# The causal mask moved from TensorE into VectorE's row maximum, and ten heads' decay falls moved from ScalarE to GpSimd

## The chip, the cores and the metric

The kernel runs on one core of a Trainium2 chip. The metric is the device time of one execution in microseconds (us). TensorE, VectorE (DVE), ScalarE (ACT) and GpSimd (POOL) each take their instructions in program order, and SyncE (SP) issues the loads and stores.

## The reference

One step of a hybrid decoder layer: latent attention with 8 heads and a Mamba-2 mixer with 16 state-space heads read the same normalised input (512 prompt tokens and 8 sample tokens, width 1024). What the change touches:

```python
# attention of the prompt, by head and by block of 128 queries
sc = (q_lat @ ckv.T + q_rope @ k_rope.T) * SOFTMAX_SCALE
sc = where(k_pos <= q_pos, sc, NEG_BIG)          # the causal mask
p  = softmax(sc)                                 # exp(sc - row maximum) / row sum
# state-space heads, chunks of 128 tokens; a_cum is the running sum of dt * a
decay_in = exp(a_cum[l] - a_cum[s]) for s <= l, else 0
y_diag   = (C B^T * decay_in) @ xdt
# then y = (y_diag + y_off + d * xs) * silu(z), and an RMSNorm over each group of 8 heads
```

## The kernel before, in words

The order of the work is written out by hand for each engine; semaphores join the engines. There are four stages: the first loads and first two weight tiles (0 to 15 us), the projections (to 279 us, with the sample tokens' paged attention woven in), the state-space states and the value matrices (to 312 us), the loop over the attention heads (312 to 397 us), and the output projection (to the end).

**First stage.** SP loads `xraw` tile by tile and the pieces 1 to 3 of the first two weight tiles; ACT's queue loads `cols` and piece 0 of both. PE runs six f32 matmuls on a zeroed tile before `first_two`. Each weight tile is split into `w_hi` (ACT, `hi`) and `w_lo` (DVE, `lo`), and PE's item i waits for `w_lo` of item i. `norm_total(0)` (L1842) sums the squares over the partitions, and ACT's `root(0, r_pre)` makes the norm's factor from it; ACT does this at i == 1, ahead of `hi(4)`.

**Head loop.** Iteration s of `for s in range(H - 1)` on every engine:

- PE: `scores(s+1)` for blocks 0, 1 and 2, the transposes `probs_t(s, 0)` and `probs_t(s, 1)` (L2067), `scores(s+1)` block 3, one `y_pair` of state-space heads (L2019, L2022; two in iteration 1, none in 6), `keys(s+2)` (L2043), and `outs(s, 0..3)` (L2075) between the last transposes. A block's scores are `kn` (f32, L2056), the mask (`ident_r` by `mask_r`, 128 columns, L2057) and two rope parts (L2058, L2059). The three PSUM banks of scores go round, so block 3 waits until ACT's `exps(s+1, 0)` has read block 0.
- DVE: `mask_max` (L1451, a row maximum in PSUM), `inverse_sum` (L1457), `head` (L1396, the decay times C B^T), `state_update` (L1416) and `dots` (L1424, a multiply and row sum with accumulator) of the sample states, `mix_low` (L1469), `y_pair` (L1404, L1405, L1406), and `gated` (L1465) last.
- ACT: `exps` (L917), the copies of `pt` and `kn`, `mix_high`, `gated_square` (L658), `state_decay` (L893), and `decays(h)`: four Relu with a bias, 128x128 each (L883), then one Exp of 128x512 (L886).
- POOL: `norm` (L1688, probabilities by the inverse row sum), `gate(t)` (L1694) and `add_square(t)` (L1705).

The decay tiles `dec` are loaded by SP (`load_acb`) once an earlier `y_pair` on PE has freed the slot. Behind the loop DVE has the chain `group_scale(0..3)` (L1480), `lo(NIN)`, `mix_low(6)`, `gated(7)`, `lo(NIN+1)`, `ssm_low(0)`, `mix_low(7)`, and PE's first output item needs its weights and, at its eighth tile, `mix_low(7)`.

Of the kernel before, what the change touches and what calls it, by code (L numbers as in the profile page):

```python
# [19 lines left out]
P = 128  # L20
# [49 lines left out]
M_ID, M_ONE, M_TRI, M_MQ, M_ML = range(5)  # L70
# [34 lines left out]
STATE_DECAYS = {0: (1,), 1: (2,), 2: (3,), 3: (4,), 4: (5,)}  # L105
# [19 lines left out]
def build(nc, a):  # L125
# [95 lines left out]
    for name, shape in (("cm", [P, 5, P]), ("cols", [P, NCOL]), ("rows", [P, 2, SH]), ("qlp", [P, 2, NB, 32 + ROWS]),  # L221
# [8 lines left out]
        if name == "cm":  # L230
            CM_ = o
        if name == "qlp":
            dxs = at("dxs", [P, 2, 8, NB], F, o)
            orow = at("orow", [P, 2 * P], F, o + 2048)
# [24 lines left out]
    nmh, alpha, rs, epsc, nmx, rsum = (small[k] for k in ("nmh", "alpha", "rs", "epsc", "nmx", "rsum"))  # L259

    ident_r = at("ident_r", [P, P], R, CM_ + 4 * P * M_MQ)
    mask_r = at("mask_r", [P, P], R, CM_ + 4 * P * M_ML)

# [29 lines left out]
    a_mask, a_gf, a_out = sem("mask_rounded"), sem("group_factor_done"), sem("out_copied")  # L293
# [97 lines left out]
    def _(sp):  # L391
# [234 lines left out]
    def _(act):  # L626
# [143 lines left out]
        for i in range(2):  # L770
            act.dma_start(w_raw[i][:, 0:256], a["w_in"][i][:, 0:256]).then_inc(s_w0[0], 16)
# [22 lines left out]
        for i in range(NIN):  # L794
# [30 lines left out]
            if i == 1:  # L825
                root(0, r_pre)
# [51 lines left out]
        def decays(h):  # L878

            act.wait_ge(s_acb[h % 6], 16 * (h // 6 + 1))  # L880
            for c in range(NCH):
                x = dec[h % 6][:, CH * c:CH * c + CH]
                last = act.activation(x, x, ACT.Relu, bias=acum[:, SH * c + h:SH * c + h + 1], scale=-1.0)  # L883
            last.then_inc(a_fall, 1)
            act.wait_ge(a_fall, h + 1)
            act.activation(dec[h % 6], dec[h % 6], ACT.Exp, scale=-1.0).then_inc(a_dec, 1)  # L886
# [23 lines left out]
        def exps(h, b):  # L910
# [6 lines left out]
            act.activation(pr[:, h % 2, i0:i0 + n], px[:, n_ % 3, 0:n], ACT.Exp, bias=nmx[:, k:k + 1], accum_out=rsum[:, k:k + 1])\  # L917
# [58 lines left out]
        for s in range(H - 1):  # L976
            exps(s + 1, 0)
            exps(s + 1, 1)
            copy_pt(s, 0)
            exps(s + 1, 2)  # L980
# [3 lines left out]
            if s in (1, 2):  # L984
                gated_square(SQUARES[s][0])
# [5 lines left out]
            if 3 <= s < 6:  # L991
                gated_square(SQUARES[s][0])
# [4 lines left out]
            if s == 6:  # L997
                gated_square(SQUARES[s][0])
# [8 lines left out]
            if s in (1, 2):  # L1007
                gated_square(SQUARES[s][1])
            for n in STATE_DECAYS.get(s, ()):
                state_decay(n)  # L1010
# [50 lines left out]
    def _(dve):  # L1061
# [471 lines left out]
        for s in range(H - 1):  # L1533
# [18 lines left out]
            if s < 6:  # L1552
                inverse_sum(s + 1, 2)
            if s in PAIRS:
                y_pair(PAIRS[s][0])
            for h in MASKS[1].get(s, ()):
                head(h)
            inverse_sum(s + 1, 3)
            if s == 6:
                group_scale(0)  # L1560
                group_scale(1)
            if s == 0:
                state_update(s)
            if s < 6:
                dots(s)
            gated(s)
# [72 lines left out]
    def _(pool):  # L1639
# [49 lines left out]

        def gate(t):  # L1690
# [19 lines left out]
        for s in range(H - 1):  # L1710
            norm(s + 1, 0)
            norm(s + 1, 1)
            for t in GATES[0].get(s, ()):
                gate(t)
            norm(s + 1, 2)
# [38 lines left out]
    def _(pe):  # L1754
# [205 lines left out]
        for _ in range(6):  # L1960
# [85 lines left out]
        def scores(h, blocks):  # L2046
            pe.wait_ge(a_ring, RING_AT["k", h] + 1)
            pe.wait_ge(v_qsl, STACK_AT[h])
            if h == 0:
                pe.wait_ge(a_mask, 2)  # L2050
                pe.wait_ge(v_krl, 1)
            for b in blocks:
# [4 lines left out]
                pe.matmul(px[:, n % 3, P * b:w], ident_r, mask_r, start=False, stop=False)  # L2057
# [139 lines left out]
def laid_out(x_prompt, x_sample, cache_ckv, cache_krope, state_conv, state_ssm, page_table, norm_pre, w_in,  # L2197
# [47 lines left out]
    out["cm"] = np.stack([ident, ones, low.T, np.where(low > 0, f(0), f(NEG)), np.where(low.T > 0, f(0), f(NEG))], 1)  # L2245
# [48 lines left out]
```

## Time and profile before

| what | us |
|---|---|
| median of 3 runs | 506.93 (506.39 to 507.68) |
| the profiled execution, its own time | 506.42 |
| span of the profile (first to last instruction) | 504.6 |
| PE busy in the span | 493.4 |
| DVE, ACT, POOL busy | 345.6, 293.4, 86.2 |
| granted TensorE clock, mean | 1.00 |

The 1.8 us between the span and the execution's own time lie outside the profile. A record of PE includes its pipelined end, so the distance from start to start tells its pace better than its duration.

### The profile page before, as it was taken

What the parts mean: (1) busy time and instruction counts of PE and PEld (TensorE: products, weight loads), DVE (VectorE), ACT (ScalarE), POOL (GpSimd) and SP (SyncE); (2) the same over time, 40 slices, a digit from 0 to 9 for tenths busy, and PEclk for the clock granted to TensorE, in tenths of its full rate; (3) what the DMA queues carried; (4) which work ended last, traced back from release to release, by engine and by line L of the source; (5) the groups of instructions that cost most, each with busy time, mean ns of one, the idle gap of its engine ahead of it and who ended that gap; (6) DMA issues with size and microseconds to landing.
All of it is one profiled execution on the core that took longest, in us unless ns stands there. A gap on an engine that the chain in (4) does not pass through costs nothing.

```text
span 504.6 us, 12857 instructions
## 1 busy us (share of the span) xinstructions
PE 493.4 (98%) x5002; PEld 440.3 (87%) x5002; DVE 345.6 (68%) x758; ACT 293.4 (58%) x616; POOL 86.2 (17%) x104
## 2 busy tenths in 40 slices
PE   8999999999999999999999999999999999999996
PEld 7999999999999998999999775666666699999994
DVE  5543768693856566644523698799997899996642
ACT  6543412234376473664616985689996879674532
POOL 1631000020010010000000132244554302110520
PEclk9999999999999999999999999999999999999999
DMA  8534223469898998989886542737435777889712
GB/s 307 197 128 150 81 65 103 132 212 357 280 332 281 308 294 286 326 278 332 298 279 185 60 130 49 255 92 123 142 95 184 229 251 230 296 270 376 242 58 84
DMA packets 58975, 105.72 MB, mean 210 GB/s; under 512 B 7722, under 2 KB 27859, under 8 KB 58787
## 3 DMA queue, kind: packets, MB, share of 16 engines
q1 hardware_dynamic: 58482, 104.59, 65.3%
q8 instruction: 40, 0.66, 0.5%
q10 hardware_dynamic: 432, 0.31, 0.2%
q14 instruction: 21, 0.16, 0.1%
HBM read 95.62 MB, written 7.76 MB: 205 GB/s over the span
## 4 chain that ended last, share of the span: by engine, by line
PE 80%; DVE 9%; ACT 6%; issue 3%; DMA 1%; SPq 0%; POOL 0%; DVEq 0%; ACTq 0%; POOLq 0%
PE pm L1757 17%; PE pm L1758 16%; PE pm L1759 16%; PE px L1868 3%; PE px L2056 3%; PE pm L2043 3%; PE px L1893 3%; PE pm L2075 3%; DVE w_lo L1077 2%; DVE u L1170 1%; PE px L2019 1%; PE pm L2022 1%; PE pm L2067 1%; ACT w_hi L641 1%; PE px L2058 1%
## 5 line engine op out<-in xcount | busy, mean ns | idle before, releaser
L1757 PE MATMUL pm<-xw_hi,w_lo 128*128 128x260 f32 x520 | 150.7, 290 | 0.9 <-DVE w_lo L1077 0.9
L1758 PE MATMUL pm<-xw_lo,w_hi 128*128 128x260 f32 x520 | 147.1, 283 | 0.0
L1759 PE MATMUL pm<-xw_hi,w_hi 128*128 128x260 f32 x520 | 146.9, 283 | 0.0
L641 ACT ACTIVATE w_hi<-w_raw 128x1024 fp32r<-128x1024 f32 (+1 forms) x70 | 72.4, 1037 | 73.2 <-PE pm L1759 61.0
L1077 DVE TENSOR_TENSOR w_lo<-w_raw,w_hi 128x1024 fp32r<-128x1024 f32 (+1 forms) x70 | 86.6, 1242 | 38.0 <-ACT w_hi L641 37.8
L1757 PEld LDWEIGHTS pm<-xw_hi,w_lo 128*128 128x128 f32 x520 | 98.0, 188 | 2.7 <-DVE w_lo L1077 1.1
L1758 PEld LDWEIGHTS pm<-xw_lo,w_hi 128*128 128x128 f32 x520 | 97.9, 188 | 0.1
L1759 PEld LDWEIGHTS pm<-xw_hi,w_hi 128*128 128x128 f32 x520 | 97.9, 188 | 0.0
L1757 PE MATMUL pm<-mix_hi,w_lo 128*128 128x260 f32 x224 | 63.8, 285 | 0.1
L1759 PE MATMUL pm<-mix_hi,w_hi 128*128 128x260 f32 x224 | 63.3, 283 | 0.0
L1757 PEld LDWEIGHTS pm<-mix_hi,w_lo 128*128 128x128 f32 x224 | 42.2, 188 | 0.6 <-DVE mixlo_a L1469 0.3
L1759 PEld LDWEIGHTS pm<-mix_hi,w_hi 128*128 128x128 f32 x224 | 42.2, 188 | 0.0
L761 ACT ACTIVATE alpha<-nmh 128x1 f32<-128x1 f32 x16 | 4.7, 295 | 56.1 <-DVE nmh L1183 56.1
L1170 DVE SCALAR_TENSOR_TENSOR u<-xbc,cols,u 128x511 f32<-128x511 f32 (+2 forms) x36 | 27.0, 750 | 7.0 <-ACT u L704 6.1
L1758 PE MATMUL pm<-mixlo_s,w_hi 128*128 128x260 f32 x112 | 31.7, 283 | 0.0
L1758 PE MATMUL pm<-mixlo_a,w_hi 128*128 128x260 f32 x112 | 31.6, 283 | 0.0
L1104 DVE TENSOR_TENSOR z<-pm,r_pre 128x260 f32<-128x260 f32 x32 | 13.5, 426 | 25.0 <-PE pm L1759 24.9
L1678 POOL TENSOR_TENSOR xdte<-xdt,toend 128x512 f32<-128x512 f32 x8 | 9.8, 1231 | 110.5 <-DVE xdt L1378 110.5
L1670 POOL COPY xlast<-xbc 128x11 f32<-128x11 f32 x12 | 6.0, 502 | 132.4 <-DVE xbc L1104 132.4
L1688 POOL TENSOR_SCALAR pr<-pr,rsum 128x128 f32<-128x128 f32 (+3 forms) x32 | 19.4, 606 | 49.4 <-DVE rsum L1457 48.7
L2056 PE MATMUL px<-kn,q 128*128 128x128 f32 (+3 forms) x64 | 23.1, 443 | 0.8 <-ACT pr L917 0.8
L1416 DVE SCALAR_TENSOR_TENSOR hring<-bcs,dxs,hring 128x128 f32<-128x128 f32 x64 | 23.1, 422 | 0.0
(314 smaller groups left out, 1081.9 us busy)
## 6 DMA issues: line engine op xcount, KB each, us to landing
page<-in_cache SPq DMA_DIRECT2D x128, 288.0 KB, 4.2
w_raw<-in_w_in SPq DMA_DIRECT2D x32, 512.0 KB, 5.5
w_raw<-in_w_out SPq DMA_DIRECT2D x32, 512.0 KB, 4.7
dec<-ac_dram SPq DMA_DIRECT2D x16, 256.0 KB, 10.0
hring<-in_ssm_state SPq DMA_DIRECT2D x8, 512.0 KB, 8.2
o_ssms<-hring SPq DMA_DIRECT2D x8, 512.0 KB, 6.7
w_raw<-in_w_qb SPq DMA_DIRECT2D x6, 384.0 KB, 2.9
xraw<-in_xT SPq DMA_DIRECT2D x8, 260.0 KB, 4.8
```

Source lines behind the costliest of these rows:

```text
L641: act.activation(w_hi[s][:, 0:n], w_raw[s][:, 0:n], ACT.Copy).then_inc(a_whi, 1)
L1077: dve.tensor_tensor(w_lo[s][:, 0:n], w_raw[s][:, 0:n], w_hi[s][:, 0:n].bitcast(F), ALU.subtract)\
L1170: last = dve.scalar_tensor_tensor(b[:, s:NT], xbc[:, t, 0:NT - s], col(C_CW + 4 * t + 3 - s), b[:, s:NT], ALU.mult, ALU.add)
L1416: dve.scalar_tensor_tensor(hring[b][:, t, :], bcs[b % 2][:, g, :], dxs[:, 0, t, b:b + 1], hring[b][:, t, :], ALU.mult, ALU.add).then_inc(v ...
L1688: pool.tensor_scalar(x, x, rsum[:, k:k + 1], 0.0, ALU.mult, ALU.add).then_inc(g_n, 1)
L1757: pe.matmul(out, wl, xh, start=start, stop=False)
L1758: pe.matmul(out, wh, xl, start=False, stop=False)
L1759: return pe.matmul(out, wh, xh, start=False, stop=stop)
L1868: last = pe.matmul(px[32 * j:32 * j + 32, n % 2, 64 * half:64 * half + 64], w, pages[s][:, j, c:c + 64], start=op == 0, stop=op == 4)
L1893: last = pe.matmul(px[32 * j:32 * j + 32, 3, 0:KVR], ptb[:, n % 2, c:c + 32], pages[page_slot(2 * n + half)][:, j, 0:KVR], start=half == 0 ...
L2043: last = pe.matmul(out, w_uk[:, h % 2, r, :], ckv[:, r, 0:NT], start=r == 0, stop=r == 1)
L2056: pe.matmul(px[:, n % 3, 0:w], q[:, h, P * b:P * b + P], kn[:, h % 2, 0:w], start=True, stop=False)
```

## The change

- The mask's matmul L2057 is gone (32 of them), and with it the two rounding activations on ACT and two of the five matrices in `cm`. A new tile `over` (128x512: zeros, then the triangle of -1e30) is loaded by SP after page 16, ahead of the second decay load. `mask_max` becomes one `tensor_tensor_reduce` over the block: it writes -(score + mask) back to PSUM in place and accumulates the minimum; `exps` takes the scores with scale -1.
- For heads 6 to 15 the four subtractions (`fall`) run on POOL; ACT keeps the Exp and waits for them. A fall stands at the start and at the end of POOL's iterations 1 to 4, one at the end of iteration 0, and two at the end of iteration 1.
- The order in the loop: POOL's gates and additions stand between `norm(s+1, 1)` and `norm(s+1, 2)`; the additions 6 and 7 come after the loop. DVE does `inverse_sum(s+1, 2)` and `y_pair` ahead of `mix_low` and `head`, then `state_update`, `dots`, `gated`; in iteration 6 `gated` stands ahead of `group_scale(0)` and `(1)`. ACT does `state_decay` ahead of `exps(s+1, 2)`, and all squares after `mix_high`.
- At the start: five dummy matmuls, not six; piece 0 of the first weights goes to SP's queue behind `xraw[0]`; `root(0, r_pre)` stands behind `hi(4)` (i == 2).

```diff
-SQUARES = {1: (0, 1), 2: (2, 3), 3: (4,), 4: (5,), 5: (6,), 6: (7,)}
-GATES = {1: (1,), 2: (3,)}, {0: (0,), 1: (2,), 2: (4,), 3: (5,), 4: (6,), 5: (7,)}
-ADDS = {1: (1,), 2: (2,), 3: (3,), 4: (5,), 5: (6,), 6: (7,)}
+SQUARES = {1: (0,), 2: (1,), 3: (2, 3), 4: (4,), 5: (5,), 6: (6,)}
+GATES = {0: (0,), 1: (1,), 2: (2, 3), 3: (4,), 4: (5,), 5: (6,)}
+ADDS = {2: (1,), 3: (2,), 4: (3,), 5: (5,), 6: (6,)}
...
+            if k == 0:
+                for i in range(2):
+                    sp.dma_start(w_raw[i][:, 0:256], a["w_in"][i][:, 0:256]).then_inc(s_w0[0], 16)
...
+        sp.dma_start(over, a["over"]).then_inc(s_over, 16)
...
-            if i == 1:
+            if i == 2:
                 root(0, r_pre)
...
+            else:
+                act.wait_ge(g_fall, h - 5)
+                act.activation(dec[h % 6], dec[h % 6], ACT.Exp).then_inc(a_dec, 1)
...
-            dve.tensor_reduce(nmx[:, 4 * (h % 2) + b:4 * (h % 2) + b + 1], x[:, 0:P * (b + 1)], AX.X, ALU.max,
-                              negate=True).then_inc(v_m, 1)
+            dve.tensor_tensor_reduce(x, x, over[:, NT - w:NT], -1.0, -NEG, ALU.add, ALU.min,
+                                     nmx[:, 4 * (h % 2) + b:4 * (h % 2) + b + 1]).then_inc(v_m, 1)
...
+        def fall(h):
+
+            pool.wait_ge(s_acb[h % 6], 16 * (h // 6 + 1))
+            for c in range(NCH):
+                x = dec[h % 6][:, CH * c:CH * c + CH]
+                last = pool.tensor_scalar(x, x, acum[:, SH * c + h:SH * c + h + 1], 0.0, ALU.subtract, ALU.min)
+            last.then_inc(g_fall, 1)
...
         for s in range(H - 1):
+            if s == 6:
+                pool.wait_ge(v_dot, 24)
+                gate(7)
+            for h in FALLS[s][0] if s in FALLS else ():
+                fall(h)
             norm(s + 1, 0)
             norm(s + 1, 1)
-            for t in GATES[0].get(s, ()):
+            for t in GATES.get(s, ()):
                 gate(t)
+            if s < 6:
+                for t in ADDS.get(s, ()):
+                    add_square(t)
             norm(s + 1, 2)
             norm(s + 1, 3)
-            for t in GATES[1].get(s, ()):
-                gate(t)
-            for t in ADDS.get(s, ()):
-                add_square(t)
+            for h in FALLS[s][1] if s in FALLS else (6,) if s == 0 else ():
+                fall(h)
+        add_square(6)
+        add_square(7)
...
-        for _ in range(6):
+        for _ in range(5):
...
-                pe.matmul(px[:, n % 3, P * b:w], ident_r, mask_r, start=False, stop=False)
```

## Rows read from the trace of the kernel before

**Rows 1.** Page, busy times; window table: PE, PEld, DVE, ACT, POOL, clock, DMA.
```profile
PE 493.4 (98%) x5002; PEld 440.3 (87%) x5002; DVE 345.6 (68%) x758; ACT 293.4 (58%) x616; POOL 86.2 (17%) x104
...
360.00:370.00 10.00, 10.00 (x58) 6.80 (x52) 9.00 (x26) 9.03 (x29) 4.98 (x6) 1.00 0.49 103
```

**Rows 2.** PE's timeline in the head loop: start, duration, instruction.
```profile
318.37 0.39 PE L2056 MATMUL px<-kn,q 128*128 128x128 f32 x2
...
354.13 0.39 PE L2056 MATMUL px<-kn,q 128*128 128x128 f32 x2
...
357.76 1.10 PE L2056 MATMUL px<-kn,q 128*128 128x512 f32 x2 [0.25 <-ACT pr L917]
...
376.50 0.39 PE L2056 MATMUL px<-kn,q 128*128 128x128 f32 x2
376.64 0.31 PE L2057 MATMUL px<-mask_r,ident_r 128*128 128x128 f32 x1
376.78 0.28 PE L2058 MATMUL px<-kr_lo,qs 128*128 128x128 f32 x1
376.89 0.28 PE L2059 MATMUL px<-kr_hi,qs 128*128 128x128 f32 x1
...
379.70 1.02 PE L2056 MATMUL px<-kn,q 128*128 128x512 f32 x2
...
388.30 0.38 PE L2056 MATMUL px<-kn,q 128*128 128x128 f32 x2
```

**Rows 3.** PE's waits over the whole span: total, times, longest.
```profile
PE pm L1757 <- DVE w_lo L1077: 0.9, 1, 0.9
PE px L2056 <- ACT pr L917: 0.8, 3, 0.4
```

**Rows 4.** Timelines of POOL, ACT, DVE and PE from 20 to 32 us.
```profile
20.17 6.45 POOL L1661 TENSOR_TENSOR sqs<-sqs,sqb 128x520 f32<-128x520 f32 x4
...
29.36 1.99 ACT L641 ACTIVATE w_hi<-w_raw 128x1024 fp32r<-128x1024 f32 x2
...
30.45 1.23 DVE L1077 TENSOR_TENSOR w_lo<-w_raw,w_hi 128x1024 fp32r<-128x1024 f32 x1 [5.78 <-ACT w_hi L641]
...
31.73 0.39 PE L1757 MATMUL pm<-xw_hi,w_lo 128*128 128x260 f32 x1 [0.88 <-DVE w_lo L1077]
```

**Rows 5.** The chain that ended last, at the start: start, time, what.
```profile
1.61 5.31 PE px L1962 x12
6.92 0.48 PE pm L1808 x4
```

**Rows 6.** DVE's timeline in iteration 3, and one row without POOL beside it.
```profile
369.16 1.26 DVE L1416 SCALAR_TENSOR_TENSOR hring<-bcs,dxs,hring 128x128 f32<-128x128 f32 x4
...
372.29 0.75 DVE L1404 SCALAR_TENSOR_TENSOR xbc<-xbc,cols,px 128x512 f32<-128x512 f32 x1 [0.53 <-PE pm L2022]
...
375.01 0.30 DVE L1424 CUSTOM_DVE_ANT_0 prod<-hring,bcs 128x128 f32<-128x128 f32 x1
...
375.24 0.68 DVE L1424 CUSTOM_DVE_ANT_0 prod<-hring,bcs 128x128 f32<-128x128 f32 x1
...
375.86 1.35 DVE L1424 CUSTOM_DVE_ANT_0 prod<-hring,bcs 128x128 f32<-128x128 f32 x1
...
416.93 1.14 DVE L1416 SCALAR_TENSOR_TENSOR hring<-bcs,dxs,hring 128x128 f32<-128x128 f32 x4
```

**Rows 7.** POOL's timeline in iteration 3, and its 128x128 scalings as a group.
```profile
368.82 1.20 POOL L1688 TENSOR_SCALAR pr<-pr,rsum 128x128 f32<-128x128 f32 x2 [1.41 <-DVE rsum L1457]
...
375.76 1.29 POOL L1694 TENSOR_TENSOR xbc<-xbc,z 128x512 f32<-128x512 f32 x1
...
L1688 POOL TENSOR_SCALAR pr<-pr,rsum 128x128 f32<-128x128 f32 x8 | 3.0, 372 | 20.0 <-DVE rsum L1457 20.0
```

**Rows 8.** DVE's timeline behind the head loop.
```profile
394.76 1.85 DVE L1480 SCALAR_TENSOR_TENSOR xbc<-xbc,cols,r_pre 128x512 f32<-128x512 f32 x2
...
403.02 0.69 DVE L1469 TENSOR_TENSOR mixlo_a<-u,mix_hi 128x512 fp32r<-128x512 f32 x1
```

More of the change, by code:

```diff
@@ L68 @@
 NCOL = 98
-M_ID, M_ONE, M_TRI, M_MQ, M_ML = range(5)
+M_ID, M_ONE, M_TRI = range(3)
 T_E0, T_E1 = range(2)
@@ L220, in build @@
     small = {}
-    for name, shape in (("cm", [P, 5, P]), ("cols", [P, NCOL]), ("rows", [P, 2, SH]), ("qlp", [P, 2, NB, 32 + ROWS]),
+    for name, shape in (("cm", [P, 3, P]), ("dxs", [P, 2, 8, NB]), ("cols", [P, NCOL]), ("rows", [P, 2, SH]), ("qlp", [P, 2, NB, 32 + ROWS]),
                         ("qr", [P, NB, 32]), ("ckbc", [P, 2, KVR]), ("olT", [P, 2, 2, P]),
@@ L229, in build @@
         small[name] = at(name, shape, F, o)
-        if name == "cm":
-            CM_ = o
         if name == "qlp":
-            dxs = at("dxs", [P, 2, 8, NB], F, o)
+            over = at("over", [P, NT], F, o)
             orow = at("orow", [P, 2 * P], F, o + 2048)
@@ L259, in build @@
     nmh, alpha, rs, epsc, nmx, rsum = (small[k] for k in ("nmh", "alpha", "rs", "epsc", "nmx", "rsum"))
-    ident_r = at("ident_r", [P, P], R, CM_ + 4 * P * M_MQ)
-    mask_r = at("mask_r", [P, P], R, CM_ + 4 * P * M_ML)
+    dxs = small["dxs"]
     def col(c):
@@ L878, in decays @@
         def decays(h):
[L880 to L886, printed above, removed]
+            if h < 6:
+                act.wait_ge(s_acb[h % 6], 16)
+                for c in range(NCH):
+                    x = dec[h % 6][:, CH * c:CH * c + CH]
+                    last = act.activation(x, x, ACT.Relu, bias=acum[:, SH * c + h:SH * c + h + 1], scale=-1.0)
+                last.then_inc(a_fall, 1)
+                act.wait_ge(a_fall, h + 1)
+                act.activation(dec[h % 6], dec[h % 6], ACT.Exp, scale=-1.0).then_inc(a_dec, 1)
+            else:
+                act.wait_ge(g_fall, h - 5)
+                act.activation(dec[h % 6], dec[h % 6], ACT.Exp).then_inc(a_dec, 1)
         def state_decay(n):
@@ L916, in exps @@
             i0, n, k = poff(b), P * (b + 1), 4 * (h % 2) + b
-            act.activation(pr[:, h % 2, i0:i0 + n], px[:, n_ % 3, 0:n], ACT.Exp, bias=nmx[:, k:k + 1], accum_out=rsum[:, k:k + 1])\
+            act.activation(pr[:, h % 2, i0:i0 + n], px[:, n_ % 3, 0:n], ACT.Exp, bias=nmx[:, k:k + 1], scale=-1.0, accum_out=rsum[:, k:k + 1])\
                .then_inc(a_p, 1)
@@ L983, in _ @@
                 mix_high(s - 1)
-            if s in (1, 2):
-                gated_square(SQUARES[s][0])
+            for t in SQUARES.get(s, ()):
+                gated_square(t)
             if s in FALLS:
@@ L1545, in _ @@
             mask_max(s + 1, 3)
+            if s < 6:
+                inverse_sum(s + 1, 2)
+            if s in PAIRS:
+                y_pair(PAIRS[s][0])
             if s:
@@ L1558, in _ @@
             inverse_sum(s + 1, 3)
+            if s < 6:
+                state_update(s)
+                dots(s)
+            gated(s)
             if s == 6:
@@ L1561, in _ @@
                 group_scale(1)
[L1562 to L1566, printed above, removed]
             if s == 1:
@@ L1688, in norm @@
             pool.tensor_scalar(x, x, rsum[:, k:k + 1], 0.0, ALU.mult, ALU.add).then_inc(g_n, 1)
+        def fall(h):
+            pool.wait_ge(s_acb[h % 6], 16 * (h // 6 + 1))
+            for c in range(NCH):
+                x = dec[h % 6][:, CH * c:CH * c + CH]
+                last = pool.tensor_scalar(x, x, acum[:, SH * c + h:SH * c + h + 1], 0.0, ALU.subtract, ALU.min)
+            last.then_inc(g_fall, 1)
         def gate(t):
@@ L2244, in laid_out @@
     low = np.tril(ones)
-    out["cm"] = np.stack([ident, ones, low.T, np.where(low > 0, f(0), f(NEG)), np.where(low.T > 0, f(0), f(NEG))], 1)
+    out["cm"] = np.stack([ident, ones, low.T], 1)
+    out["over"] = np.concatenate([np.zeros((P, NT - P), f), np.where(low > 0, f(0), f(NEG))], 1)
     out["swap"] = ident[np.arange(P) ^ ROWS]
```

35 lines of the change are left out of this document (10 added, 25 removed).

## The prediction

> **What bounds the kernel now.** I read the page's busy times first, then a window table by stage, then PE's timeline in the head loop, then PE's waits, then DVE's and POOL's timelines side by side. The page gives PE 98% of the span, and inside the loop PE is busy throughout while DVE and ACT stand at 90% and POOL at 50% [rows 1]. PE has hardly a wait: one of 0.9 us at 31 us and three before block 3 of the scores, 0.8 us together [rows 3]. So PE's own work sets the time, and what leaves PE is a gain only as long as the three other engines follow. In the loop they follow closely: PE's block 3 waits until `exps(s+1, 0)` has freed a bank, and that depends on how early DVE reaches `mask_max(s+1, 0)`. From the start of an iteration to block 3 it takes 3.20 us in iteration 5, without a wait, and 3.63 us in iteration 3, with one [rows 2]; a wait shown as 0.25 costs 0.43 us. The iterations 0 to 5 take 388.30 - 318.37 = 69.93 us [rows 2]; the three waits are 0.8 us, some 1.3 us by that ratio, so without any they would take 68.6.
>
> **The start.** PE's item 4 stands 0.88 us for `w_lo`; DVE made it at 30.45, behind ACT's `w_hi` at 29.36 [rows 4], and ACT came to that only behind `root`. With `root` behind `hi(4)`, which ACT, idle for 8 us before, can do as soon as PE has used item 0's weights, the wait goes: -1.0 us with the restart. One dummy matmul less: the twelve records of six took 5.31 us, 0.885 each, and real work began as they ended [rows 5]. Per column they run at half the pace of the matmuls behind them (four of 260 columns in 0.48), so some of the time won would be run at the lower pace: I take half, -0.45 us, between 0 and 0.6. The upper end is POOL's sum of squares, ended at 20.17 + 6.45 = 26.62 [rows 4], which `norm_total(0)` needs. The two loads moved to SP's queue stand behind `xraw[0]` and push the others by two issues; the queues are full by then, so I cost that at nothing; if ACT had no slack there, the 0.45 would be gone. Start: -1.5 us.
>
> **The mask on PE.** In block 0 four matmuls stand 0.14, 0.14, 0.11 and 0.11 us apart [rows 2]. One of 128 columns costs 0.11 next to its neighbours; 0.14 is the upper bound, and half of 0.11 the lower, if its weights' load was the hidden part. I take 0.11: 32 x 0.11 = 3.5 us, 0.44 a head. One head's share lies before the loop (-0.44), six heads' in it (68.6 - 2.6 = 66.0 us without waits), and the last head's lies ahead of DVE's chain behind the loop and is worth nothing by itself.
>
> **The mask on DVE.** The reduction becomes a product-like operation with an accumulator. The trace has it only as `dots`: 0.30 us for 128 columns [rows 6], start to start 0.21, about what the reduction takes at that width. It has no such operation with a 512-column block in PSUM; the neighbour of that width, L1404, takes 0.75 [rows 6] against 0.69 for the reduction. So 0 to +0.1 us each; I take 0. The load of `over` (256 KB) and the two activations gone from ACT lie where nothing waits for them.
>
> **The falls.** ACT loses 10 x 4 Relu, some 13 us, in a loop where it is 90% busy. It gives PE little by itself, since DVE is what comes late. POOL gains 40 `tensor_scalar` of 128x128, 0.37 us each alone [rows 7]: 1.4 to 1.5 us a fall, three quarters of the iterations' second half. ACT then waits for POOL in order, with `exps` of the next head behind it. What POOL's work does to DVE is the crux. When POOL runs a 1.29 us gate at 375.76, the `dots` product that DVE starts at 375.86 takes 1.35 instead of 0.30; behind a 512-column norm it takes 0.68 [rows 6, 7]. Against short ones the loss is small: four `state_update` take 1.26 with the norms of blocks 0 and 1 beside them and 1.14 alone, while the two norms take 1.20 [rows 6, 7]. I take 0.11 us for each POOL operation of 128 columns, 0.4 for norm 3, and the full length for a gate or an addition that coincides with a DVE operation of two SBUF inputs.
>
> The Trainium skill has a rule that speaks against this change (SBUF — State Buffer, "Who interferes with whom"): a DVE instruction with two SBUF inputs and a GpSimd instruction that reads SBUF exclude each other, and the later one fully blocks. The rows of the long operations agree; by the rule, short ones too would exclude each other fully, and the sum would be that of the second rival. `mask_max` has one SBUF input and is left alone by it.
>
> **The order on DVE.** Behind `y_pair` DVE now has mix_low 0.60, head 0.60, inverse_sum 0.1, state_update 1.07, dots 0.85, gated 0.6, behind 1.85 of `y_pair`: 5.67 us. In an iteration of 10.5 us `y_pair` is ready at 6.26 (scores 2.1, transposes 0.76, block 3 1.4, PE's pair 1.8, 0.2 to DVE). So DVE comes to the next `mask_max` 1.46 us into the next iteration without contention, and PE waits from about 2.06 on (mask_max 0.3, exps 0.35 and hand-over 0.1 before 2.86). A fall (4 x 0.11) and norm 3 (0.4) make it 2.3: a stall of 0.25 in each of iterations 3, 4 and 5, and 0.3 in iteration 2 (two pairs, two falls). Iteration 0 keeps 0.65 from `y_pair(0)`, whose place is as before, and iteration 1 some 0.1. Beyond that the long ones: in iteration 2 gates 2 and 3 and addition 1 stand in a row (addition 1 waits for a square made in the same iteration) just when DVE does L1406, mix_low and head, worth up to 2.2 us; in iteration 3 addition 2 likewise, up to 1.1. My times are no better than half an operation there, so I take half: 1.65. Stalls: 0.65 + 0.1 + 0.3 + 0.75 + 1.65 = 3.45. Loop: 66.0 + 3.45 - 69.93 = -0.5 us.
>
> **Behind the loop.** Before, DVE did two `group_scale` while it waited for PE's `outs(6)`, and the chain from 394.76 to the end of `mix_low(7)` at 403.7 was dense [rows 8]; its end lies 15.4 us after 388.30, and PE stood ready for it. Now `gated(6)` waits first, at 7.15 us, and all four `group_scale` come behind: 7.15 + 0.6 + 2.64 + 4.74 = 15.1 without contention. Two additions of POOL beside them cost up to 1.55; half of it gives 15.85: +0.45 us, between -0.35 and +1.25.
>
> **Sum.** -1.5 - 0.44 - 0.5 + 0.45 = -2.0 us against the profiled execution of 506.42 (span 504.6 and 1.8 around it), which is 0.5 below the median of the runs. On the median: 504.9 us.
>
> **Rivals.**
> - DVE in time: the clashes don't happen, since POOL has done gates and additions while DVE waits for PE. Only the 0.65 of iteration 0 stays: loop 66.65 - 69.93 = -3.3, behind it -0.35, in all -5.6: 501.3. For it: POOL's gates are due in DVE's idle time around block 3. Against: three additions wait for a square of the same iteration.
> - Full exclusion: short operations block too, and every long one hits. Stalls 5.8, loop +1.9, behind it +1.25, sum +1.2: 508.1. For it: 1.35 against 0.30 [rows 6]. Against: the four state updates that lost 0.12.
> - Slower, ACT behind POOL: a fall's operation at 0.68, as the norm of block 1 has it under contention (1.20 for two, 0.37 the first, a start 0.15 later), makes a fall 2.7 us. The one at the iteration's end is then done at 13.0, its Exp at 13.6, `exps` of the next head some 0.75 us late, 1.7 with two falls, and POOL at 10 us of work in an iteration of 10.5 carries lateness on: some 1.5 a time in iterations 3 to 5. Stalls 8.5, loop +4.6, sum +3.1: 510.0. It decides from about 0.5 us for each operation of a fall. For it: POOL is the only engine that gets work in each iteration, and its queue is in order before ACT's. Against: 0.37 alone.
> - The mask's matmul was hidden behind weight loads, and only half its price is won: 506.6.
>
> **How the numbers follow.** A measurement of this kernel tells about 0.3% (1.5 us) from no change. Chances: forecast 0.38 (its own range 502.5 to 507), DVE in time 0.18, full exclusion 0.22, ACT behind POOL 0.16, mask hidden 0.06. Faster than 505.4: 0.18 and most of the forecast, 0.48. Slower than 508.4: ACT behind POOL and a part of full exclusion, 0.23. Between: 0.29. The range of 8 in 10 takes in both outer cases in the main: 500.9 to 509.6.
>
> **What the profile after would show.** Right: no wait at item 4 of the projections; block 0 of the scores 0.11 us shorter; L1424-like products and L1406, mix_low and head longer than alone where POOL runs a gate or an addition; iteration 3 the longest of those with one pair; `group_scale` later and PE's stall at the eighth tile of the first output item. Wrong: iterations near 10.5 us throughout (then DVE had room and the first rival holds), or ACT idle with GpSimd named as the releaser (the third). A reduction with accumulator that takes clearly over 0.75 us at 512 columns would break the step that costs it at nothing.

## The result: slower by 1.8%, where 0.4% faster was forecast

The changed kernel takes 515.9 us (median of 4 runs, 515.0 to 517.3) against 507.1 for the kernel before on the same chip: 8.8 us between the medians. The ratio of their times is put at 1.0181, 95% interval 1.0165 to 1.0197 (the quotient of the medians is 1.0173). The forecast was 504.9, and its range ended at 509.6. The third rival, ScalarE behind GpSimd, names what happened, at 510.0 too small.

The page after has PE busy for 491.9 us, 1.5 less than before [rows 1], in a span 8.1 us longer. GpSimd has 32 us of new work:

```profile
span 512.7 us, 12820 instructions
...
PE 491.9 (96%) x4968; PEld 436.9 (85%) x4968; DVE 342.5 (67%) x790; ACT 280.9 (55%) x574; POOL 118.5 (23%) x144
```

Next, PE's timeline of the kernel after (start, duration, instruction), the rows that answer to [rows 2]: the first block of the scores of heads 0, 1, 3, 4 and 7, and one block 3.

```profile
312.53 0.39 PE L2064 MATMUL px<-kn,q 128*128 128x128 f32 x2
...
317.85 0.39 PE L2064 MATMUL px<-kn,q 128*128 128x128 f32 x2
...
342.67 0.39 PE L2064 MATMUL px<-kn,q 128*128 128x128 f32 x2
...
348.43 2.04 PE L2064 MATMUL px<-kn,q 128*128 128x512 f32 x2 [2.72 <-ACT pr L915]
...
357.47 0.39 PE L2064 MATMUL px<-kn,q 128*128 128x128 f32 x2
...
395.18 0.38 PE L2064 MATMUL px<-kn,q 128*128 128x128 f32 x2
```

The start has given nothing (scores(0) at 312.53; 312.60 before). The six iterations take 395.18 - 317.85 = 77.3 us, 7.4 more than before, and the stretch behind them 512.7 - 395.18 = 117.5, 1.2 more than 504.6 - 388.30. The head loop is the whole story, and the list of its waits (318 to 396 us: total, times, longest) says who is late:

```profile
ACT dec L884 <- POOL dec L1688: 20.7, 6, 4.0
...
PE px L2064 <- ACT pr L915: 8.8, 6, 2.7
```

Read it from the bottom: PE waits 8.8 us before block 3, in each of the six iterations, for an `exps` of ScalarE; and ScalarE itself stood 20.7 us for a fall of GpSimd. GpSimd's timeline from the end of iteration 1 on:

```profile
340.76 9.79 POOL L1688 TENSOR_SCALAR dec<-dec,acum 128x128 f32<-128x128 f32 x12
350.52 0.83 POOL L1681 TENSOR_SCALAR pr<-pr,rsum 128x128 f32<-128x128 f32 x2
351.32 2.52 POOL L1695 TENSOR_TENSOR xbc<-xbc,z 128x512 f32<-128x512 f32 x2
353.78 1.29 POOL L1706 TENSOR_TENSOR gacc<-sq,sq 128x512 f32<-128x512 f32 x1
```

All its falls as one line's instructions (duration in ns: minimum, median, maximum):

```profile
L1688 POOL TENSOR_SCALAR dec<-dec,acum x40: 708/712/1216, 329.0 to 384.8; 128x128 f32<-128x128 f32 x40
```

A fall's operation takes 0.71 us, not the 0.37 of the norm's operation of the same shape [rows 7]. Three falls in a row hold GpSimd for 9.79 us, over the turn from iteration 1 to 2. At 0.71 each the twelve operations would take 8.5 us; most of the rest is VectorE. Where one of its 512-column products of two inputs has started first, the fall's operation takes up to 1.22 us (timelines of VectorE and GpSimd):

```profile
345.32 0.69 DVE L1390 TENSOR_TENSOR dec<-dec,cbt 128x512 f32<-128x512 f32 x1
345.37 1.22 POOL L1688 TENSOR_SCALAR dec<-dec,acum 128x128 f32<-128x128 f32 x1
```

ScalarE's queue meanwhile:

```profile
343.75 0.63 ACT L884 ACTIVATE dec<-dec 128x512 f32<-128x512 f32 x1 [3.34 <-POOL dec L1688]
347.31 0.63 ACT L884 ACTIVATE dec<-dec 128x512 f32<-128x512 f32 x1 [2.93 <-POOL dec L1688]
347.85 0.35 ACT L915 ACTIVATE pr<-px,nmx 128x128 f32<-128x128 f32 x1
```

The last row is the `exps` for which PE waits at 348.43. Its input lay ready (VectorE's maximum was done at 345.1), but it stood in order behind two exponentials whose falls weren't made. TensorE's granted clock fell too, in the stretch in which PE sat idle for 2.72 us and just behind it (windows: busy times, PEclk, DMA share):

```profile
318.00:346.00 28.00, 26.23 (x162) 17.93 (x160) 22.88 (x73) 15.48 (x44) 18.80 (x26) 1.00 0.62 176
346.00:354.00 8.00, 5.57 (x29) 3.27 (x30) 2.82 (x10) 6.24 (x18) 8.00 (x11) 0.79 0.69 123
354.00:395.00 41.00, 36.35 (x196) 23.29 (x195) 33.37 (x105) 23.66 (x66) 34.82 (x41) 1.00 0.37 98
```

0.79 is a mean over time at 2.4 and at 1.2 GHz. It is why the row at 348.43 lasts 2.04 us instead of 1.10 [rows 2]. The other iterations kept 1.00.

### The profile page after: what moved, and what is told of

Its sections match the earlier page's. It is cut to its first block, busy times and chain, and to the rows that moved or that the text cites. A ratio compares the mean times of both kernels' runs of the same rounds, so it can differ in the third digit from the quotient of the medians.

```text
span 512.7 us, 12820 instructions
## 1 busy us (share of the span) xinstructions
PE 491.9 (96%) x4968; PEld 436.9 (85%) x4968; DVE 342.5 (67%) x790; ACT 280.9 (55%) x574; POOL 118.5 (23%) x144
## 4 chain that ended last, share of the span: by engine, by line
PE 68%; DVE 11%; POOL 7%; ACT 6%; issue 4%; DMA 2%; SPq 1%; ACTq 0%; DVEq 0%; POOLq 0%
PE pm L1766 16%; PE pm L1767 16%; PE pm L1768 16%; POOL dec L1688 4%; PE px L1877 3%; PE px L1902 3%; PE px L2064 2%; POOL sqs L1654 2%; DVE u L1164 1%; PE px L2028 1%; DVE w_lo L1071 1%; PE pm L2031 1%; DVE dec L1390 1%; PE pm L2052 1%; ACT w_hi L642 1%
## 5 line engine op out<-in xcount | busy, mean ns | idle before, releaser
L2064 PE MATMUL px<-kn,q 128*128 128x128 f32 (+3 forms) x64 | 24.3, 462 | 8.8 <-ACT pr L915 8.8
L1688 POOL TENSOR_SCALAR dec<-dec,acum 128x128 f32<-128x128 f32 x40 | 30.7, 784 | 0.0
L1681 POOL TENSOR_SCALAR pr<-pr,rsum 128x128 f32<-128x128 f32 (+3 forms) x32 | 21.2, 665 | 25.0 <-DVE rsum L1453 25.0
```

The lines of the kernel that those rows point to most:

```text
L1681: pool.tensor_scalar(x, x, rsum[:, k:k + 1], 0.0, ALU.mult, ALU.add).then_inc(g_n, 1)
L1688: last = pool.tensor_scalar(x, x, acum[:, SH * c + h:SH * c + h + 1], 0.0, ALU.subtract, ALU.min)
L2064: pe.matmul(px[:, n % 3, 0:w], q[:, h, P * b:P * b + P], kn[:, h % 2, 0:w], start=True, stop=False)
```

## The experiments

Each was run 5 to 12 times beside the kernel before, except fall_forms, which is one execution and stands outside the table. The ratios are not quotients of the medians and can differ from them by 0.1%. Differences of times below are differences of medians; the kernel before had medians of 506.9 to 507.1 beside the various runs. The table gives from each profile: the start of scores(0), the six iterations, iteration 3, and the stretch behind them. Two kernels whose first 300 us are the same code (loads_back, scale_first) differ by 1.5 us at scores(0), so single figures of that column carry that much.

| kernel | scores(0) | loop | iteration 3 | behind | us | ratio (95%) |
|---|---|---|---|---|---|---|
| before | 312.6 | 69.9 | 11.4 | 116.3 | 507.1 | 1 |
| after | 312.5 | 77.3 | 12.3 | 117.5 | 515.9 | 1.0181 (1.0165-1.0197) |
| fall_cheap | 312.7 | 71.4 | 14.2 | 117.9 | 509.6 | 1.0050 (1.0031-1.0069) |
| falls_on_act | 312.6 | 69.4 | 12.2 | 117.5 | 507.4 | 1.0010 (0.9995-1.0025) |
| falls_only | 312.3 | 80.2 | 12.9 | 116.3 | 517.1 | 1.0198 (1.0179-1.0218) |
| mask_only | 312.1 | 69.4 | 11.4 | 116.5 | 506.0 | 0.9992 (0.9977-1.0006) |
| mask_start | 311.4 | 69.4 | 11.4 | 116.0 | 504.7 | 0.9957 (0.9944-0.9970) |
| loads_back | 312.6 | 69.5 | 12.4 | 117.5 | 506.7 | 0.9991 (0.9979-1.0003) |
| scale_first | 311.1 | 69.3 | 12.2 | 117.6 | 505.8 | 0.9983 (0.9972-0.9993) |
| decay_early | 311.7 | 69.5 | 11.8 | 116.1 | 505.0 | 0.9962 (0.9946-0.9978) |
| few_falls | 311.2 | 69.2 | 11.8 | 116.0 | 504.6 | 0.9944 (0.9927-0.9960) |
| adds_out | 311.9 | 69.3 | 12.2 | 116.4 | 504.9 | 0.9953 (0.9937-0.9969) |
| state_late | 311.3 | 72.8 | 15.4 | 117.6 | 506.9 | 0.9999 (0.9983-1.0015) |
| best_order | 311.3 | 69.9 | 12.8 | 116.6 | 505.8 | 0.9974 (0.9962-0.9986) |
| mixed_order | 312.0 | 70.4 | 13.3 | 116.5 | 506.3 | 0.9999 (0.9985-1.0012) |

### fall_forms: what a fall's operation costs, by its form

```diff
-                last = pool.tensor_scalar(x, x, acum[...], 0.0, ALU.subtract, ALU.min)
+                last = pool.tensor_scalar(x, x, acum[...], 0.0, op0, op1)   # one form for each head, widths 128, 256, 512
```

> The changed kernel, with another form of GpSimd's operation for each of the ten heads 6 to 15 (two operations of the instruction and the width differ, the operands stay; the decays of these heads come out as 1). Theory A, the form sets the price: the forms without a comparison (subtract and add, mult and add, add and add, mult and subtract) take 0.37 us for 128 columns as the norm does, those with a minimum or a maximum 0.71. Rival A2, subtraction is what is dear: the forms with a subtraction take 0.71, mult with min 0.37. Rival B, contention or the place in the queue is what makes them slow: all forms take about 0.7. For 256 and 512 columns of subtract and min, a price per element gives 1.3 and 2.5 us, a fixed price per instruction 0.87 and 1.2.

Theory A and both its rivals fell. GpSimd's timeline: one operation of head 6 (subtract and add), one of head 7 (mult and min), one of head 8 (mult and add), head 10 at 256 columns, head 9 at 512.

```profile
330.52 0.71 POOL L1692 TENSOR_SCALAR dec<-dec,acum 128x128 f32<-128x128 f32 x1
...
334.09 0.71 POOL L1692 TENSOR_SCALAR dec<-dec,acum 128x128 f32<-128x128 f32 x1
...
341.13 0.40 POOL L1692 TENSOR_SCALAR dec<-dec,acum 128x128 f32<-128x128 f32 x1
...
342.52 2.00 POOL L1692 TENSOR_SCALAR dec<-dec,acum 128x512 f32<-128x512 f32 x1
...
347.62 1.14 POOL L1692 TENSOR_SCALAR dec<-dec,acum 128x256 f32<-128x256 f32 x1
```

Of the eight pairs tried at 128 columns only mult and add, the norm's, is cheap; subtract with add, mult with min, add with min, subtract with max, add with add, mult with subtract and min with add all take 0.71 to 0.74 where nothing stretches them. It is neither the comparison nor the subtraction, and not the place in the queue either. Per column the dear form costs (2.00 - 1.14) / 256 = 3.4 ns. In time: 513.5 us.

### fall_cheap and falls_on_act: the change at the assumed price, and without the falls

```diff
-                last = pool.tensor_scalar(x, x, acum[...], 0.0, ALU.subtract, ALU.min)
+                last = pool.tensor_scalar(x, x, acum[...], 0.0, ALU.mult, ALU.add)   # fall_cheap
```

fall_cheap's ten decays are other numbers than the kernel's, and ScalarE's Exp there has a scale of -1 (the edit's other line). falls_on_act takes `decays` from the kernel before (four Relu and an Exp on ScalarE for every head) and drops `fall`.

> The changed kernel with the fall's operations as multiply and add (as the norm's) in place of subtract and minimum, the rest as it is; the decays of heads 6 to 15 are wrong values for it. It gives the change at the price that the prediction assumed. Theory A (a fall's operation at 0.71 us, with ACT queued behind it, is the whole of the miss): a fall takes 1.5 us, the waits of ACT for GpSimd go, and the kernel comes to 503 to 506 us. Rival B (contention): the operations still take about 0.7 and the kernel stays at 515 to 516. Rival C (the new order on VectorE costs more than I priced): operations at 0.37 but the kernel at 508 to 512.

> The changed kernel with the falls of heads 6 to 15 back on ScalarE as before; mask, order and start stay as changed. Theory A: the mask is worth 3.5 us less some stalls, so 503.5 to 506 us. Rival C (the new order costs by itself): 508 us or more. A ScalarE that is at 90% could also be late for block 3, then 506 to 508.

At the assumed price the kernel takes 509.6, 6.3 us less than the changed kernel (0.0131 of the ratio's 0.0181): that is what the operation's form costs. The time lies in rival C's band, which the next kernel narrows: without falls it takes 507.4, a further 2.2 less, in the band named for a late ScalarE and short of rival C's. Falls at 0.37 still cost that. Nearly all of it lies in iteration 3 (14.2 us against 12.2), where they delay the gates and the addition behind them. In fall_cheap GpSimd runs addition 1 from 350.42 on, for 1.58 us; VectorE's timeline beside it:

```profile
350.79 1.75 DVE L1465 TENSOR_TENSOR mixlo_a<-u,mix_hi 128x512 fp32r<-128x512 f32 x1
```

`mix_low` takes 1.75 instead of 0.68, ScalarE waits until 355.89 for a fall, and iteration 3 becomes 14.2 us. About 1.3 of these 2.0 us are the clock: its mean in this iteration is 0.88, and PE's work takes 12.27 us instead of 10.96. And mask, order and start together are worth nothing: 507.4 against 506.9, where 3.5 us of mask and 1.5 of start had been promised.

### falls_only: the falls without the rest

```diff
             norm(s + 1, 3)
+            for h in FALLS[s][1] if s in FALLS else (6,) if s == 0 else ():
+                fall(h)
             for t in GATES[1].get(s, ()):
```

> The kernel before with the falls of heads 6 to 15 on GpSimd and nothing else of the change; each fall stands in GpSimd's queue where the changed kernel has it. Theory A: ScalarE waits for GpSimd as in the changed kernel and the kernel loses more than the whole change does, since no mask pays it back: 516 to 520 us. Rival C: 507 to 509, as the falls alone do little.

517.1 us, 10.2 more than before, as theory A has it. Together with falls_on_act it closes the sum: falls +10.2 alone and +8.5 on top of the rest (515.9 less 507.4), the rest between +0.5 (falls_on_act) and -1.2 (515.9 less 517.1).

### mask_only and mask_start: where the mask's gain goes

mask_only is the kernel before with `over`, the new `mask_max` and the scores without the mask's matmul. mask_start adds one line:

```diff
-            if i == 1:
+            if i == 2:
                 root(0, r_pre)
```

> The kernel before with the mask in VectorE's row maximum and nothing else of the change: order, start and falls as before. Theory D (the mask's matmuls are PE's own time, and VectorE keeps up in the old order): scores(0) 0.44 us earlier, each iteration 0.3 to 0.44 shorter, 503.5 to 504.5 us. Rival E (VectorE's queue sets the pace, so what PE saves at the mask it waits at block 3): 506 to 507.3, with more wait before block 3 than the 0.8 us of before.

> mask_only with the root of the input's norm behind the rounding of item 4's weights (root at i == 2), the loads and the dummy matmuls as before. By the prediction's term the 0.9 us wait of item 4 goes and the end comes 0.9 to 1.0 us earlier than mask_only's. Theory F (VectorE's w_lo for item 4 now runs while GpSimd sums squares, and the two exclude each other): GpSimd's four sums take 7.2 instead of 6.45 us, PE waits for them at norm_total about 0.3 us, and 0.3 to 0.6 us of the gain stay.

Rival E holds, and PE's waits before block 3 add up to 2.1 us instead of 0.8. Ahead of the loop the mask gives what was forecast: from scores(0) to scores(1) 5.31 us instead of 5.77. Inside it gives 0.5 us of 2.6. Iteration 4 has no listed wait in either kernel and is still only 0.13 shorter (10.81 against 10.94). PE's timeline of mask_only there:

```profile
364.39 0.39 PE L2050 MATMUL px<-kn,q 128*128 128x128 f32 x2
...
366.50 0.93 PE L2060 MATMUL pm<-cm,pr 128*128 128x128 f32 x7
367.50 1.10 PE L2050 MATMUL px<-kn,q 128*128 128x512 f32 x2
```

PE's timeline before, in the same iteration:

```profile
365.56 0.39 PE L2056 MATMUL px<-kn,q 128*128 128x128 f32 x2
...
368.00 0.93 PE L2067 MATMUL pm<-cm,pr 128*128 128x128 f32 x7
368.77 1.02 PE L2056 MATMUL px<-kn,q 128*128 128x512 f32 x2
```

There the transposes began 368.00 - 365.56 = 2.44 us into the iteration and block 3 followed 0.77 behind them. In mask_only they begin at 2.11, 0.33 earlier (three blocks at 0.11), and block 3 comes 1.00 behind: 0.23 of the 0.33 has turned into waiting. ScalarE's timeline of mask_only shows for what:

```profile
363.91 1.27 ACT L876 ACTIVATE dec<-dec,acum 128x128 f32<-128x128 f32 x4
365.21 0.63 ACT L879 ACTIVATE dec<-dec 128x512 f32<-128x512 f32 x1
365.75 1.27 ACT L886 ACTIVATE hring<-hring,dxs 128x128 f32<-128x128 f32 x4
366.92 0.35 ACT L910 ACTIVATE pr<-px,nmx 128x128 f32<-128x128 f32 x1
```

VectorE had the maximum by 365.99, but ScalarE first finishes the fall, the exponential and `state_decay`, 3.0 us without a gap. PE had been arriving just as ScalarE was done. The new row maximum itself is as cheap as forecast: 0.70 us for 512 columns in the kernel after, against 0.69 for the reduction.

mask_start takes 504.7, 1.3 less than mask_only: the wait of 0.9 us at item 4 is gone. In the two profiles 0.7 us of the gain is there at scores(0); another 0.5 lies behind the loop, in code that is the same, and so is not the root's. Theory F is right in its mechanism: the sums of GpSimd stretch, and PE waits 0.3 us for them.

```profile
19.97 7.25 POOL L1656 TENSOR_TENSOR sqs<-sqs,sqb 128x520 f32<-128x520 f32 x4
```

They took 6.45 before [rows 4]. In the thirteen kernels that have the root moved they take 7.22 to 7.38, in the three without 6.45.

### loads_back and scale_first: the start's loads, and the order behind the loop

```diff
         act.dma_start(cols, a["cols"]).then_inc(s_cols, 16)
+        for i in range(2):
+            act.dma_start(w_raw[i][:, 0:256], a["w_in"][i][:, 0:256]).then_inc(s_w0[0], 16)
```

scale_first also swaps `gated(6)` and the first two `group_scale` back.

> falls_on_act with the two loads of the first weights back on ScalarE's queue (one dummy matmul less and the root behind item 4's rounding stay). Theory F (moving them delayed the input's pieces, and with them the squares): ScalarE starts the squares near 14.6 us instead of 15.2, GpSimd's sums end at 27.4 instead of 28.0, PE's wait at norm_total falls from 1.2 to 0.6, and the span is 0.5 to 0.6 us shorter than falls_on_act's 504.8. Rival (the loads cost nothing): no change in these.

> loads_back with VectorE's group_scale(0) and (1) in front of gated(6), as before the change. Theory G (the order behind the loop costs the 1.2 us that the stretch from the last scores to the end grew by): the stretch comes back to about 116.5 us, and PE's two waits of 0.7 us behind the loop go. Rival: the place of group_scale costs nothing and the stretch stays at 117.5; what costs is GpSimd's two additions or the gates.

In loads_back ScalarE starts the squares at 14.31, the sums end at 27.16, and PE's listed wait for them is gone, as theory F has it; the span is 0.2 longer than falls_on_act's all the same, as a page load of the cache came late in that profile (0.5 us, absent in scale_first). The comparison that carries it is over all kernels: with the two loads on SyncE's queue (four kernels) the squares start at 15.04 to 15.29, with them on ScalarE's (twelve) at 13.87 to 14.68.

Theory G fell: with `group_scale` ahead the stretch behind the loop is still 117.6. VectorE's timeline of scale_first:

```profile
394.29 2.83 DVE L1470 SCALAR_TENSOR_TENSOR xbc<-xbc,cols,r_pre 128x512 f32<-128x512 f32 x2
```

And GpSimd's:

```profile
393.20 3.38 POOL L1692 TENSOR_TENSOR sqs<-sqs,sq 128x512 f32<-128x512 f32 x2
```

Two `group_scale` take 2.83 instead of 1.85 [rows 8] beside two additions, and these 3.38 instead of some 2.6 (two of 1.3). That made theory J.

### decay_early and few_falls: relieving ScalarE at the iteration's end

```diff
             copy_pt(s, 0)
+            if 0 < s < 5:
+                state_decay(s + 1)                 # decay_early
```
```diff
+            if 2 <= s <= 4:
+                fall(POOL_FALLS[s - 2])            # few_falls: heads 11, 13, 15, in iterations 2 to 4
             norm(s + 1, 2)
```

> mask_start with ScalarE's state_decay of the groups 2 to 5 half an iteration earlier (behind copy_pt(s, 0) in iterations 1 to 4, in place of the end of the iteration); VectorE's and GpSimd's order as before. Theory H (in the old order it is ScalarE's queue at the iteration's end, decays 1.9 us and state_decay 1.27, that keeps exps(s+1, 0) late, so that the mask's saving turns into wait before block 3): exps(s+1, 0) comes up to 0.7 us earlier in iterations 2 to 5, the waits of 0.54 and 0.63 us before block 3 go, and the kernel comes to 503 to 503.8 us. Rival: VectorE's row maximum, 1.25 us into the iteration, is the next limit so closely behind that at most 0.5 us come off, or the four activations push exps(s+1, 2) and the wait appears later in the iteration: 504.2 to 505.

> mask_start with the falls of the heads 11, 13 and 15 alone on GpSimd, between the second and the third norm of iterations 2 to 4, where GpSimd is idle for 1.8 to 2.1 us; ScalarE keeps the other thirteen. A fall takes 2.9 us there; the third norm comes 0.9 us late, in iteration 2 some 1 to 2.5 us, with 2.8 us to spare until PE's transposes. Theory H: ScalarE is 1.27 us sooner at exps(s+1, 0) in iterations 3 to 5, without a wait for GpSimd, and the kernel comes to 503 to 504 us. Rival (any fall at GpSimd's price delays its gates and additions, and these VectorE and PE): 505 to 507.

decay_early is at mask_start's time (505.0 and 504.7): its rival holds, `exps` now waits 0.51 us for VectorE in iterations 4 and 5. few_falls is the fastest kernel measured, 504.6, though not apart from mask_start, and between the bands of its theory and its rival. A fall there takes 3.0 to 3.3 us and nobody waits for it:

```profile
357.70 3.28 POOL L1696 TENSOR_SCALAR dec<-dec,acum 128x128 f32<-128x128 f32 x4
```

So the dear fall is no harm where its user comes half an iteration later. It gives little, since VectorE is next: in iteration 3 `exps` waits 1.68 us for VectorE's maximum, and PE 1.07 instead of 0.63.

### adds_out, state_late, best_order, mixed_order: what the new order loses

```diff
-            pool.tensor_tensor(total, ..., ALU.add)
+            pool.tensor_tensor(total[:, 0:w], ..., ALU.add)      # adds_out: w = 8 for t = 2, 3, 6, 7
```
```diff
-            if t == 1:
+            if t == 2:                            # state_late, best_order: 512 KB load later in SyncE's queue
                 load_state(2)
```
```diff
+            if s == 2:                            # mixed_order
+                mix_low(s - 1)
+                state_update(s)
             if s in PAIRS:
                 y_pair(PAIRS[s][0])
```

> loads_back with four of GpSimd's six additions of squares (t = 2, 3, 6, 7) cut from 512 to 8 columns, so that the group norm's factor is not the reference's; queue, waits and the rest stay. Theory J (GpSimd's long additions of two inputs lie beside VectorE's mix_low and behind the loop beside group_scale, and block it): iteration 3 shrinks from 12.2 to about 11.1 us, the stretch behind the loop from 117.5 to about 116.5, and the kernel comes to 504.5 to 505. Rival: these stay within 0.3 us of loads_back's, and the order of VectorE's own work is what costs.

> loads_back with one load moved: the 512 KB load of state group 2 is issued one step later in SyncE's queue (t == 2 in place of t == 1), so that it no longer stands ahead of the decays' sums of heads 10 and 11 and of ea(4). Theory K (what is left of the order's loss in iteration 3 is VectorE standing at y_pair(4) for the load of ea, 1.2 to 2.4 us in loads_back, scale_first and adds_out, because y_pair now comes before mix_low and state_update): the wait for ea goes, iteration 3 shrinks from 12.4 to 11.0 to 11.4 us, and the kernel comes to 505.2 to 505.8. Rival: the load of ea is late because its issue waits for PE's and VectorE's previous pair, not for the queue ahead of it; then the wait and iteration 3 stay.

> state_late with the two causes of the tail undone as well: group_scale(0) and (1) ahead of gated(6) as before the change, and GpSimd's addition 6 between its third and fourth norm of iteration 6, where it stands idle, so that only addition 7 lies beside group_scale. If theories J (behind the loop) and K hold, the stretch behind the loop is 116.4 to 116.8 us and the kernel comes to 503.5 to 504.5; if the order is no better than the old one in any place, it ends at mask_start's 504.7 or above.

> best_order with the state load back at its place, and in iteration 2 alone VectorE's mix_low(1) and state_update(2) ahead of y_pair(4), as before the change; elsewhere the changed kernel's order. Theory L (what makes iteration 3 long is that the new order leaves VectorE with nothing to do in iteration 2 before y_pair(4), whose inputs, PE's pair and the load of ea, come 1.3 to 4.4 us after the last row maximum): the idle time is filled, iteration 3 takes 11.0 to 11.4 us in place of 12.2 to 15.4, and the kernel comes to 503.0 to 504.0. Rival: the wait is only moved, since y_pair(4) and with it GpSimd's gate still come late; iteration 3 stays above 12 and the kernel at 505.5 to 506.

Theory J is half right. Behind the loop the additions are the cost: 116.4 without them, and 116.6 in best_order, where addition 6 sits in a gap; the six of the table with both additions there have 117.5 to 117.9. (The old order gives 116.0 to 116.5, in one profile each.) Iteration 3 stays long, 12.2. adds_out keeps addition 1, which GpSimd runs in iteration 2, from 348.84 to 350.11. VectorE's timeline beside it:

```profile
349.19 1.34 DVE L1394 TENSOR_TENSOR xbc<-xbc,yt 128x384 f32<-128x384 f32 x1
```

That is 0.56 alone. VectorE's timeline of loads_back in iteration 2 shows another wait:

```profile
346.65 0.70 DVE L1441 CUSTOM_DVE_ANT_0 px<-px,over 128x512 f32<-128x512 f32 x1
...
349.62 0.75 DVE L1392 SCALAR_TENSOR_TENSOR xbc<-xbc,cols,px 128x512 f32<-128x512 f32 x1 [1.82 <-DMA ea<-ea_dram]
```

`y_pair(4)`, put first behind the maximum, finds the load of `ea` not landed, and nothing else is in front of it. With the 512 KB load moved (theory K) the wait was 4.4 us in state_late and 2.4 in best_order, so K fell: the wait doesn't go with that load. state_late's profile is of an execution of 508.8 us, 1.9 above its median: PE stood 2.16 us and the iteration's clock was 0.89. best_order, at 505.8, stays above mask_start, as its expectation has it for an order that is better nowhere. Filling the idle place in mixed_order moved the loss:

```profile
347.92 1.62 DVE L1459 TENSOR_TENSOR mixlo_a<-u,mix_hi 128x512 fp32r<-128x512 f32 x1 [0.74 <-ACT mix_hi L922]
349.47 2.47 DVE L1404 SCALAR_TENSOR_TENSOR hring<-bcs,dxs,hring 128x128 f32<-128x128 f32 x4
```

Both are twice as long as alone, beside gates 2 and 3 and addition 1, which the change put in one row in iteration 2. Theory L fell and its rival holds in the main: iteration 3 stays above 12 us, the kernel ends 0.3 above the rival's band. Six profiles have the late load, of 1.1 to 4.4 us, and three (falls_on_act, adds_out, mixed_order) the clash alone. (The expectation of state_late counts adds_out with the first; in the profile read here its load was in time.)

Neither is the 0.8 us that iteration 3 takes more in falls_on_act (12.18) than in mask_start (11.36). Before block 3 PE waits 0.59 us in the one and 0.63 in the other. What is new is a second wait, further on. Timelines of ScalarE and PE in falls_on_act:

```profile
357.40 1.27 ACT L886 ACTIVATE hring<-hring,dxs 128x128 f32<-128x128 f32 x4
...
360.01 1.15 ACT L658 ACTIVATE sq<-xbc 128x512 f32<-128x512 f32 x2
...
363.56 0.59 ACT L901 ACTIVATE kn<-pm 128x512 f32<-128x512 f32 x1
...
364.20 0.33 PE L2057 MATMUL pm<-cm,pr 128*128 128x128 f32 x1 [0.63 <-ACT kn L901]
```

PE's last transpose of the head waits until ScalarE has copied `kn` out of its bank. ScalarE is without a gap from 356.07 on, and the changed order has put `state_decay` (1.27) and two squares (1.15) between `exps(s+1, 0)` and this copy; it starts 10.5 us into the iteration instead of 9.1. With 0.23 us more of PE's own work (10.96 against 10.73) the 0.63 makes up the 0.8. The same wait, of 0.62 to 0.64 us, stands in loads_back, scale_first, adds_out, best_order and mixed_order. In those of them with a longer iteration 3 the wait before block 3 is longer too (0.82 in loads_back, 1.15 in mixed_order, 1.18 in best_order): there the late load and the clash come in. No run puts ScalarE's order alone back, so this reading is of the rows and not of an experiment.

## Why the prediction was wrong, step by step

- **The step that failed: the price of a fall.** "0.37 us per operation" was taken from the norm's row as the nearest of the same opcode and shape. The fall's pair of operations made it 0.71: a fall is 2.9 us, not 1.5, and with VectorE's products in its way 3.1 on the mean of the ten (31.4 us). The rival priced just this (0.68, deciding from 0.5), but for another reason (contention) and with a chance of 0.16. At 0.37 the kernel takes 509.6 instead of 515.9, so 6.3 us come from this term. Of the 10.8 us between forecast and result another 2.2 are what the falls cost even at 0.37, and some 2.5 are mask, order and start, which were to give 2.0 us (falls included) and lost 0.5 without any fall.
- **ACT behind POOL** was the right mechanism, with the right place. It was forecast as stalls of some 1.5 us in iterations 3 to 5 and a loop of +4.6. Measured: +7.4, with the largest wait in iteration 2, where two iteration-end falls and the next iteration's first stand in one row; the lower clock there is part of it (12.08 us of PE's work in that iteration against 10.7 in iterations 3 and 4).
- **The mask on PE.** The unit was right (0.11 a block, -0.46 ahead of the loop against -0.44), the product wrong: 6 heads gave 0.5 us, not 2.6. I had read "hardly a wait" as room. Block 3 at 3.21 us meant that PE and ScalarE arrived together.
- **The mask on DVE** at nothing: right.
- **The order on DVE.** Loop -0.5 in the sum, -0.6 measured in falls_on_act: equal by chance, made of other parts. VectorE's arrival at the next maximum was forecast at 1.46 us and is 1.73 in iteration 5 of falls_on_act. The clash of additions in iterations 2 and 3 was foreseen; that VectorE would stand idle in front of `y_pair(4)`, with a DMA next in line, was not, nor was PE's wait of 0.6 us for the copy of `kn`, which comes of the new order on ScalarE. That order has no term in the sum. Two small slips in the working change little: 6.26 + 5.67 - 10.5 is 1.43, and 2.86 less 0.75 is 2.11.
- **Contention** between falls and VectorE was priced at 0.11 for each, as a loss of VectorE, and that was right: beside falls a `dots` product takes 0.28 to 0.40. Full exclusion of VectorE, the second rival, is wrong for them. The other direction was priced at nothing and wasn't: behind a 512-column product of VectorE a fall's operation takes 1.22 instead of 0.71, in all 2.9 of the falls' 31.4 us. (The rows of groups 6 and 7 up to 376 us lie in iteration 4, 365.56 to 376.50, not 3; no term hangs on it.)
- **The start.** -1.5 forecast, none measured. The wait at item 4 did go, but the loads "at nothing" delayed the squares by 0.9 us on the mean of the kernels (15.2 against 14.3), and the earlier `w_lo` took 0.8 from GpSimd's sums, so that PE stood 1.1 us at `norm_total(0)`. I had given that end as a bound for the dummy matmul (26.62) and had not asked what moves it.
- **Behind the loop.** +0.45 forecast, +1.2 measured, inside the bound of 1.25, by the mechanism named (two additions).

What is fastest is the mask and the root of the change in the old order, without or with three falls in a gap: mask_start at 504.7 and few_falls at 504.6 us, 2.3 to 2.5 us less than before.

## What to carry to other kernels

Price an operation by its own form, not by its opcode and shape; where the trace has no row of that form, the range must reach to the price at which an engine in the queue becomes the bound. Put a producer's work half an iteration ahead of its user: ten falls at the turns of the iterations cost 10 us, three in a gap half an iteration ahead nothing. And where the busiest engine shows almost no wait, look at how long ago its releaser finished before you count its saved work as saved time.

## What the runs showed of the hardware

- GpSimd's `tensor_scalar` with mult and add takes 0.37 us for 128 columns and, with no product of VectorE beside it, 0.69 for 512 (0.8 ns a column; 0.72 to 0.90 beside VectorE's state updates); with any of seven other pairs 0.71 for 128, and with subtract and min 1.14 for 256 and 2.00 for 512 (3.4 ns a column). The Trainium skill (GPSIMD Engine Reference, "Engine selection") says that one-input operations run there at roughly line rate; the norm's form agrees, the others don't.
- Beside GpSimd's operations of one tensor input and 128 columns VectorE's two-input products lost 0.1 us for each, whether it took 0.71 us (changed kernel) or 0.37 (fall_cheap); beside the 512-column norm 0.4 (0.68 instead of 0.28); beside two-input ones (gates, additions) they took up to 1.35 instead of 0.30. It goes both ways: VectorE's `w_lo` (1.2 to 2.2 us) cost GpSimd's sums 0.8, and its 512-column product a fall's operation 0.5. The Trainium skill (SBUF — State Buffer, "Who interferes with whom") has a full block for any GpSimd operation that reads SBUF; the rows agree for the long ones of two inputs and nearly (0.5 of 0.69 us) for a fall behind a product, and not for a product behind a fall.
- The wait before block 3 costs more than itself: in the iterations in which PE stood idle there for 1.90, 2.16, 2.72 and 3.31 us (fall_cheap, state_late, after, falls_only) the mean granted clock was 0.88 or 0.89, and PE's own work took 12.1 to 12.7 us instead of 10.7 to 11.2. In those with a wait of 1.74 or less it stayed at 1.00.
